# The place of TensorE's branch in the expert stages: behind the gather, or behind 28 matmuls of the first gate product

## Time and profile before

| | |
|---|---|
| median of 3 runs | 1905.83 us (1903.82 to 1909.61) |
| the profiled execution, its own time | 1907.05 us |
| its span, first to last instruction | 1905.3 us |
| TensorE busy | 1842.3 us (97%) |
| weight loads | 1191.4 us (63%) |
| VectorE, ScalarE, GpSimd busy | 570.0, 362.2, 15.8 us |
| DMA | 592.16 MB, mean 311 GB/s |
| first expert stage | from about 866 us to about 1321 us |
| second expert stage | from about 1438 us to about 1894 us |

### The profile page before, as it was taken

How to read it: one execution, slowest core, us unless ns; L and a number is a source line. 1 busy time by engine, 2 the same in 40 slices (tenths; PEclk the granted TensorE clock), 3 DMA queues, 4 the chain that set the end, 5 groups by cost and what they waited for, 6 DMA issues and landing times.

```text
span 1905.3 us, 22711 instructions
## 1 busy us (share of the span) xinstructions
PE 1842.3 (97%) x9422; PEld 1191.4 (63%) x9422; DVE 570.0 (30%) x1288; ACT 362.2 (19%) x809; POOL 15.8 (1%) x31
## 2 busy tenths in 40 slices
PE   8999999999999999999999998999999999988998
PEld 7798888957988888575444433335885444433333
DVE  3279550432655703433111110112133111110112
ACT  3440000322301003433211110112013121111111
POOL 1000000000001000000000000000000000000000
PEclk9999999999999999999999999999999999999999
DMA  9846676432377762339999999999567999999996
GB/s 295 278 177 251 273 305 253 188 132 89 133 286 295 300 244 89 133 121 355 414 426 428 429 432 432 432 426 428 204 242 274 407 424 427 430 433 431 431 428 257
DMA packets 53550, 592.16 MB, mean 311 GB/s; under 512 B 6082, under 2 KB 20810, under 8 KB 23890
## 3 DMA queue, kind: packets, MB, share of 16 engines
q1 hardware_dynamic: 52882, 588.74, 75.7%
q10 hardware_dynamic: 576, 2.10, 0.3%
HBM read 585.34 MB, written 1.05 MB: 308 GB/s over the span
## 4 chain that ended last, share of the span: by engine, by line
PE 79%; DMA 18%; DVE 2%; ACT 1%; issue 0%; DVEq 0%; SPq 0%; ACTq 0%
PE ps L548 28%; PE ps L1262 17%; DMA ring<-in_w_up 16%; PE ps L789 8%; PE ps L1384 6%; PE ps L1221 3%; PE ps L1214 2%; PE ps L618 2%; PE ps L835 1%; DMA ring<-in_w_down 1%; PE ps L707 1%; PE ps L650 1%; PE ps L636 1%; PE ps L996 1%; PE ps L1449 1%; PE ps L1036 1%
## 5 line engine op out<-in xcount | busy, mean ns | idle before, releaser
L548 PE MATMUL ps<-hsq,ring 128*128 128x256 f32 x2048 | 447.3, 380 | 0.8 <-DVE hsq L2126 0.8
L1262 PE MATMUL ps<-ring,work 128*64 128x512 f32 x1792 | 406.3, 607 | 38.2 <-DMA ring<-in_w_up 30.7
L548 PEld LDWEIGHTS ps<-hsq,ring 128*128 128x128 f32 x2048 | 387.8, 190 | 59.5 <-issue 7.0
L1262 PEld LDWEIGHTS ps<-ring,work 128*64 128x64 f32 x1792 | 129.1, 139 | 303.8 <-issue 250.3
L1692 ACT ACTIVATE work<-ps 128x512 f32<-128x512 f32 (+2 forms) x175 | 89.7, 517 | 827.0 <-PE ps L548 325.0
L1384 PE MATMUL ps<-ring,work 128*64 128x512 f32 x864 | 191.9, 596 | 1.6 <-DMA ring<-in_w_down 1.3
L789 PE MATMUL ps<-work,ring 128*128 128x256 f32 (+1 forms) x704 | 148.5, 373 | 0.0
L2071 DVE SCALAR_TENSOR_TENSOR work<-ring,silu_c,work 128x512 f32<-128x512 f32 x196 | 143.7, 754 | 5.1
L789 PEld LDWEIGHTS ps<-work,ring 128*128 128x128 f32 x704 | 130.5, 190 | 18.7 <-issue 1.7
L2574 DVE TENSOR_TENSOR work<-ps,work 128x512 f32<-128x512 f32 x26 | 18.0, 692 | 389.2 <-ACT work L1692 389.2
L1384 PEld LDWEIGHTS ps<-ring,work 128*64 128x64 f32 x864 | 59.4, 137 | 117.6 <-issue 112.8
(11 more groups left out here) (330 smaller groups left out, 1368.4 us busy)
## 6 DMA issues: line engine op xcount, KB each, us to landing
ring<-in_w_up SPq DMA_DIRECT2D x16, 4096.0 KB, 22.0
ring<-in_w_down SPq DMA_DIRECT2D x16, 4096.0 KB, 20.4
ring<-in_w_gate SPq DMA_DIRECT2D x16, 4096.0 KB, 21.4
ring<-in_w_ada SPq DMA_DIRECT2D x24, 2048.0 KB, 9.2
ring<-in_w_gate SPq DMA_DIRECT2D x24, 2048.0 KB, 12.6
ring<-in_w_up SPq DMA_DIRECT2D x22, 2048.0 KB, 16.1
ring<-in_w_down SPq DMA_DIRECT2D x22, 2048.0 KB, 18.2
ring<-in_w_ff_gate SPq DMA_DIRECT2D x10, 2048.0 KB, 13.6
```

The source lines that it names most:

```text
L548: last = mm(ps[:, b, 0:T], w[:, k, m * P:(m + 1) * P], rhs[:, k, :], start=(i == 0), stop=(i == nk - 1))
L1262: last = mm(ps[e * CAP:(e + 1) * CAP, w, :], xg[:, k, e * CAP:(e + 1) * CAP], tile_of(first, w, i, 2 * k // KT, e, k % HTL), start=(k == 0 ...
```

## The change

The first seven steps of pair 0's gate product leave the place ahead of the branch and go, with the eighth, to the head of the Else part. The branch now follows the `value_load` and the two `open_bank` calls. The semaphores, the matmuls and their order on TensorE are the same in the part that runs. The variable `last_k` keeps its default, so that the product is closed by its eighth step alone. The diff is complete.

```diff
@@ experts(l) on TensorE @@
                 gather(e_, 1)
                 turn.take(S["crowd_ready"])
                 most = pe.value_load(crowd[0:1, 0:1])
-                pe.wait_ge(e_["xg_ready"], 1)
-                for k in range(KT - 1):
-                    if k == KT // 2:
-                        pe.wait_ge(e_["xg_ready"], 2)
-                    if k in (0, KT // 2):
-                        half_arrived(first, 0, 0, 2 * k // KT)
-                    last = gate_step(first, 0, 0, k, last_k=KT - 2)
-                    if k in (1, 3):
-                        last.then_inc(e_["gate_half"], 1)
                 for b in (0, 1):
                     open_bank(b)
                     owner[b] = None
                 with pe.If(most > CAP):
@@ gathered_tokens(e_, first) @@
-                product_of(0, 0, KT - 1, e_["gate_full"])
+                pe.wait_ge(e_["xg_ready"], 1)
+                for k in range(KT):
+                    if k == KT // 2:
+                        pe.wait_ge(e_["xg_ready"], 2)
+                    if k in (0, KT // 2):
+                        half_arrived(first, 0, 0, 2 * k // KT)
+                    last = gate_step(first, 0, 0, k)
+                    if k in (1, 3):
+                        last.then_inc(e_["gate_half"], 1)
+                last.then_inc(e_["gate_full"], 1)
                 turn_weights(0)
```

## The result

The kernel after took 1912.80 us (median of 10 runs, 1909.16 to 1914.50), the kernel before 1905.07 us in the 10 runs that stand beside it. The ratio is 1.0038, with a 95% interval of 1.0029 to 1.0046: 5.5 to 8.8 us slower. The forecast was 1913.0. The profiled executions are 5.5 us apart (1912.60 against 1907.05; spans 1910.8 against 1905.3).

A forecast was written before the change was run, and what follows sets the result against it. TensorE, busy 97% of the span, was taken to bound the kernel. Head 1.95, page 4.55 and clock 0.7 gave +7.2 us in the first stage, 0 in the second: 1913.0 us, range 1907.5 to 1917.

The forecast's parts named there:

- The mechanism: TensorE's branch to the Else part: the jump fetches its target's page, which 28 matmuls hid before the change.
- Part 1: Head of each stage: the branch delays the gate product by 1.95 us in the first, 2.1 in the second.
- Part 2: Page boundary behind the jump: first stage loses 4.55 us to the next page; second stage's 2.15 us hole closes.
- Part 3: TensorE after its idle time: a lower granted clock costs 0.7 us, bounds 0 and 1.8, once.
- Part 4: From first stage to the end: SyncE's loads wait for TensorE's products, so the delay passes on one for one.
- Rival C: Waits for transfers behind 1070 swallow the late start: +0, 1905.8 us; chance 0.05.
- The sum: Whole kernel: first stage +7.2 us, second stage 0; median forecast 1913.0 us.
- B: First stage: next page is no obstacle, only heads cost; +2.0 us, or +4.1 if second hole stays; chance 0.20.
- D: TensorE's branch is no fetch; its sequencer waits for the array's matmuls: 0 to -2.15 us; chance 0.07.

The follow-up runs named there:

- E1: Kernel after, with 16 entries added at the end of the first stage's all-tokens part, which does not run; 1910.0 us, ratio to before 1.0024.
- E2: Kernel before, with 64 entries added at the end of the second stage's all-tokens part, which does not run; 1903.51 us, ratio 0.9988.
- E3: Kernel before, with 172 entries added at the end of the first stage's all-tokens part, shifting both stages; 1905.65 us, ratio 1.0002.
- E4: Kernel before, gathered and all-tokens parts exchanged in TensorE's stream, so the gathered part follows the branch and ends with a jump; 1906.27 us, ratio 1.0003.
- E5: Kernel after without TensorE's branch, the all-tokens part left out for TensorE; 1902.18 us, ratio 0.9990.
- E8: Kernel before, with 16 of the gate product's matmuls ahead of the branch and 16 behind it; 1903.57 us, ratio 0.9993.
- E6: Kernel after, with SyncE's 1 MB load ahead of the branch moved behind the two quarters of the up weights; 1909.31 us, ratio 1.0025.
- E7: Kernel before, with the two quarter loads of pair 1's up weights issued behind the whole gate product; 1905.69 us, ratio 1.0008.

## Why the prediction was right

**The mechanism** held step by step; the sizes of Parts 1 to 3 did not. The jump fetches a page; the fetch was hidden behind 28 matmuls and is not behind the gather; in the first stage the move put the target 11 entries ahead of a page's end, and the array stopped behind exactly 5 matmuls; in the second it closed the hole. E1, E2 and E3 show the page's part by shifting code alone, E4 and E5 the jump's, and E8 the cover. The Trainium skill, "Runtime: NRT & Kernel Launch", section Instruction fetch mechanics, says that a taken branch out of the resident blocks waits for a fetch; E4 agrees: 0.08 to 0.09 us in order, 3.57 and 6.26 us by a jump.

**Part 1, the head,** was too small for the first stage: 1.95 forecast, 3.38 measured, outside the bound of 2.5. The step took the branch's duration from its old place. At the new one, 2.4 us earlier, a 1 MB load was still on its way, and the packet started 2.2 us after the branch and not 0.95 (E6: moving the load gives 3.55 us for the branch; the step had 3.4). The trace of the kernel before could have told it: queue 1 filled the engines up to 876 and was still at work behind it, so that a packet asked for at 876 would have met it. The windows 870:876 and 876:878 there:

```profile
q1 hardware_dynamic: 1726, 2.17, 104.3%
...
q1 hardware_dynamic: 61, 0.37, 44.6%
```

The second stage had 2.1 forecast and 2.2 of idle time. In E1, where another packet of queue 8 was under way when the branch began, it was 2.6.

**Part 2, the page,** was too large: 4.55 forecast for the first stage, 2.03 measured (5.41 - 3.38; E1 gives 2.09). The step took 5.8 us from packet to packet, from rows of 7.3 us less something for idle engines. It was 3.1 us: with no load queued between the two packets, as in E7, that is all it takes. In the kernel after, queue 8 has no packet in 879.5:881.3 and this one in 881.4:882.4:

```profile
q8 instruction: 1, 0.02, 5.5%
```

The 2.03 us are under this step's own lower bound, 4.4 less the head's 1.95, although that bound had the next page asked for as soon as the branch is over; only head and page together, 5.4, lie within the bounds given for the stage (4.4 to 8.0). The gain in the second stage was taken at its 2.15 us of idle time; the hole cost 2.74 (20.29 - 17.55), for the reason given at the end.

**Part 3, the clock,** was 0.7 forecast and nothing in the first stage, in the kernel after, E1 and E6: the granted clock is 1.00 behind idle stretches of 3.3 and 1.4 us with 5 matmuls between them. It was 0.52 behind the 2.85 us of E4's exit. What decides between the two no run here shows, so to put the term between 0 and 1.8 was fair.

**Part 4,** that the delay reaches the end, held: +5.41 at the up product, +5.20 at the last gate or up matmul. Rival C, that the delay is given back, is out.

**The sum.** First stage 7.2 forecast, 5.4 measured in the traces; second stage 0 and +0.4, the low clock at the gather included. Over 10 runs the difference is 7.7 us, and its interval (5.5 to 8.8) holds both sums. That the forecast of 1913.0 met the median to 0.2 us is luck: Part 1 was 1.4 us too small, Parts 2 and 3 were 2.5 and 0.7 too large, and the traces account for 5.8 us where the medians differ by 7.7.

**The rivals.** B, no obstacle at the page's end in the first stage, is out for this kernel (the hole behind 5 matmuls). E1 made it come true by moving the code, and even there its +2.0 us was too little: the first stage was 3.3 us late, since the head was longer than Part 1 had it. D, that the sequencer waits for the array, is out: the branch ran on for over 3 us with the array empty, and took 0.09 us in E4 with matmuls before it.

**When the next page comes.** In the traces its packet starts 0.6 to 0.8 us after the end of the branch wherever no bulk load is queued: in both stages of the kernel after, E1, E6 and E7, and at the second exit of E4. So it looks as if it is asked for when the jump is over, and not together with the jump's page. No run here changes that, so why it is so stays open.

## What to carry to other kernels

A jump to a page that isn't at hand takes TensorE 3.3 to 4.1 us here, 4.65 behind a 1 MB load, and 6.3 with the DMA engines full; put it where matmuls that are already handed over last at least that long, and don't issue a large load just ahead of it. What runs straight behind a jump also depends on how far its target is from the end of a page: a hole of one or two microseconds marked "issue" in the middle of a uniform row of matmuls can be a sign of it, and code moved or added far away can open or close it. So a comparison of two kernels that differ by a few instructions can differ by 2 us for that reason alone; shift the code by some entries that don't run before you explain a difference of that size by the work.

## What the runs showed of the hardware that was not expected

- Instruction pages stand in the same line as bulk transfers. From the branch to its page's packet: 0.9 to 1.1 us with idle engines, 2.2 with 1 MB under way, 3.7 with the engines full (E4's first exit). From the jump's page to the next: 3.1 to 3.5 us with no load queued between; 7.3 us with 2 MB in the kernel before, and 5.9 to 7.2 in E2 and E3, whose loads are the same.
- TensorE's sequencer runs some 20 matmuls ahead of the array: when the branch started at 878.5 in the kernel before, 28 had been handed over and the ninth was running. That lead is the cover, some 4 us of it. At E4's first exit the cover was 3.6 us.
- A hole costs more than the idle time that the profile gives it: 1.42 us of idle time cost 2.0 to 2.1 us (E1), 2.15 us cost 2.74, 1.27 us cost 1.49 (E3). The matmuls behind it are not slower; they start at the usual steps, in twos 0.43 us apart. The view counts idle time from the end of the last matmul's record, 0.59 us after its start, though the next one usually starts 0.01 or 0.42 us after it. From start to start the three holes are 2.01, 2.75 and 1.87 us. The first two stand between the two matmuls of a pair, where the usual step is 0.01 us, and the third between pairs, where it is 0.42 us: that gives 2.0, 2.74 and 1.45 us, the costs above.
